# Old states of the sample group as the moving operand, with q spread out over zeros as the stationary one

## What is computed

```python
def step(s, inp):                       # s: old state (128 x 256) per sequence and head
    qc, kc, vc, gc = inp
    b = jnp.cumsum(gc, axis=1)
    ...
    o = (jnp.einsum('bhij,bjhv->bihv', a, vc)
         + jnp.einsum('bihd,bhdv->bihv', qc * jnp.exp(b), s))
    ...
o, s_new = _gla_chunked(q, k, v, glog, s0)      # 4 heads, key width 128, value width 256
o = o * lax.rsqrt(jnp.mean(jnp.square(o), -1, keepdims=True) + RMS_EPS) * gla_norm_w
o = o * jax.nn.silu(g)
```

## Time and profile before

| | us |
|---|---|
| median of 3 runs | 1268.34 (1265.9 to 1268.51) |
| the profiled execution's time | 1269.73 |
| its span, first to last instruction | 1268.0 |
| TensorE busy | 1162.3 (92%) |
| VectorE busy | 467.2 (37%) |
| ScalarE busy | 248.4 (20%) |
| HBM traffic | 454.50 MB moved, 358 GB/s over the span |
| mean granted TensorE clock | 0.991 |

### The profile page before, as it was taken

The page is one execution under the profiler, slowest core; times in us unless marked ns, Lnnn a source line. Parts: engine busy times, 40 slices in busy tenths (PEclk is TensorE's granted clock), DMA queues, the critical chain, the costliest instruction groups (busy, mean ns, idle before and its releaser), DMA issues.

```text
span 1268.0 us, 15570 instructions
## 1 busy us (share of the span) xinstructions
PE 1162.3 (92%) x6265; PEld 640.4 (50%) x6265; DVE 467.2 (37%) x796; ACT 248.4 (20%) x407; POOL 27.5 (2%) x44
## 2 busy tenths in 40 slices
PE   6999999999999999998898899989898988898884
PEld 6999999998543433433343234334333423343331
DVE  4575666665533232322222231223222222322135
ACT  4544344420211111111111111111111101110112
POOL 0000100100000000000000000000000000000001
PEclk9999999999899999999999999999999999999997
DMA  9526444692499999999999999999999999999993
GB/s 380 204 101 241 137 170 158 230 365 83 167 428 423 428 427 427 426 428 427 428 428 428 427 428 428 428 427 428 429 427 427 428 429 427 427 428 428 427 424 132
DMA packets 37945, 454.50 MB, mean 358 GB/s; under 512 B 4461, under 2 KB 4589, under 8 KB 9096
## 3 DMA queue, kind: packets, MB, share of 16 engines
q1 hardware_dynamic: 33744, 439.62, 83.0%
q0 software_dynamic: 4160, 14.29, 3.3%
HBM read 447.70 MB, written 6.31 MB: 358 GB/s over the span
## 4 chain that ended last, share of the span: by engine, by line
DMA 51%; PE 44%; DVE 3%; ACT 1%; issue 1%; SPq 0%; DVEq 0%; ACTq 0%
DMA ring<-in_w_gu 31%; DMA ring<-in_w_down 19%; PE bank L1009 13%; PE bank L706 12%; PE bank L1037 6%; PE bank L774 3%; PE bank L749 2%; PE bank L1061 1%; PE bank L982 1%; PE bank L833 1%; PE bank L820 1%; DMA ring<-in_w_mix 1%; PE bank L761 1%; DVE arena L1626 1%; PE bank L823 1%
## 5 line engine op out<-in xcount | busy, mean ns | idle before, releaser
L1009 PE MATMUL bank<-ring,arena 128*64 128x512 f32 x1504 | 339.8, 599 | 44.0 <-DMA ring<-in_w_gu 44.0
L1009 PEld LDWEIGHTS bank<-ring,arena 128*64 128x64 f32 x1504 | 103.7, 137 | 258.7 <-issue 182.8
L1037 PE MATMUL bank<-ring,arena 128*64 128x512 f32 x784 | 178.7, 598 | 18.0 <-DMA ring<-in_w_down 17.7
L706 PE MATMUL bank<-arena_r,ring_r 128*128 128x320 f32 x848 | 182.3, 316 | 0.0
L1865 DVE SCALAR_TENSOR_TENSOR arena_r<-bank,arena,arena_r 64x512 fp32r<-64x512 f32 x62 | 46.4, 749 | 289.5 <-ACT arena_r L1408 289.0
L706 PEld LDWEIGHTS bank<-arena_r,ring_r 128*128 128x128 f32 x848 | 138.7, 188 | 0.6 <-issue 0.4
L1828 DVE COPY arena<-bank 128x512 f32<-128x512 f32 x32 | 22.1, 692 | 290.6 <-PE bank L1009 290.6
L1009 PE MATMUL bank<-arena 128*64 128x512 f32 x528 | 119.8, 596 | 7.7 <-DMA arena<-in_w_gu 7.4
L1037 PEld LDWEIGHTS bank<-ring,arena 128*64 128x64 f32 x784 | 54.1, 136 | 121.9 <-issue 99.3
L1396 ACT ACTIVATE arena<-bank 128x512 f32<-128x512 f32 x32 | 19.1, 598 | 423.4 <-PE bank L1009 423.4
L1499 DVE TENSOR_TENSOR ring_r<-ring,ring_r 128x1024 fp32r<-128x1024 f32 x56 | 67.8, 1224 | 56.5 <-ACT ring_r L1225 56.3
(11 more groups left out here) (258 smaller groups left out, 957.8 us busy)
## 6 DMA issues: line engine op xcount, KB each, us to landing
ring<-in_w_gu SPq DMA_DIRECT2D x94, 2048.0 KB, 35.0
ring<-in_w_down SPq DMA_DIRECT2D x48, 2048.0 KB, 35.1
arena<-in_w_gu SPq DMA_DIRECT2D x33, 2048.0 KB, 35.2
ring<-in_w_mix SPq DMA_DIRECT2D x32, 1024.0 KB, 5.2
arena<-in_w_down SPq DMA_DIRECT2D x15, 2048.0 KB, 35.1
arena<-in_state_gla POOLq DMA_DIRECT2D x4, 1024.0 KB, 6.8
out<-arena POOLq DMA_DIRECT2D x4, 1024.0 KB, 5.6
alone<-in_w_gu SPq DMA_DIRECT2D x1, 2048.0 KB, 9.3
```

Of the source, the lines that this page charges most:

```text
L706: last = mm(o[:, 0:NT], w[a][:, c, f0:f0 + 128], rhs[b][:, c, :], start=c == 0 and a + b == 0, stop=c == chunks - 1 and a == 1)
L1009: last = mm(ex[i][side * CAP:(side + 1) * CAP, :], xgt[:, 2 * j + c, block * CAP:(block + 1) * CAP], w[:, c, i * D + side * 512:i * D + (s ...
L1037: last = mm(out[side * CAP:(side + 1) * CAP, :], actt[:, 4 * j + c, :], w[:, c, side * 512:(side + 1) * 512], start=j == 0 and c == 0, sto ...
```

## The change

The 64 small matmuls are taken out from between the chunks of the `g` products. In their place stands, behind the first `g` product of each head, a product `r` of its own: q of the 8 sequences is laid out by VectorE (`set_apart`) in a buffer of zeros, `q_apart`, so that sequence b has a block of 64 columns in which only its own 8 hold q. That block is the stationary operand (64 columns), the old state of the sequence with its 256 columns the moving one. Even sequences add up in partitions 0 to 63 of the bank, odd ones in 64 to 127. ScalarE copies the bank to SBUF (`old`), and one more matmul per half of the output (stationary 128 x 128 of `old`, moving `twice`: two 64 x 64 identity matrices one above the other) turns it and adds the two parts into the output's sample columns. The buffer of zeros lies in `alone`, so the first expert piece now waits for the last `r` and is issued behind all mixer units. `r` takes a place in `PRODUCTS`, so every bank number behind it moves on.

```diff
@@ PRODUCTS
-               [("o", h, 0), ("o", h, 1), ("g", 2 * h), ("kv", h, 0), ("kv", h, 1), ("g", 2 * h + 1)]
+               [("o", h, 0), ("o", h, 1), ("g", 2 * h), ("r", h), ("kv", h, 0), ("kv", h, 1), ("g", 2 * h + 1)]
@@ views
+        q_apart = alone[:, 0:B * NS]
+        old = reg(WRT, DV)
+        twice = reg(RMS + NT, NS)
@@ SyncE, mixer units
-                if n == 2 * RING:
-                    sp.dma_start(slot_view(-1), w_gu[0, 0, :, :]).then_inc(alone_in, 16)
@@ SyncE, behind the mixer units
+            sp.wait_ge(*full(("r", HEADS - 1)))
+            sp.dma_start(slot_view(-1), w_gu[0, 0, :, :]).then_inc(alone_in, 16)
             sp.wait_ge(stored_s, 16 * HEADS)
@@ TensorE, per head
             for h in range(HEADS):
                 outs = [claim(("o", h, vc)) for vc in range(2)]
+                weights_times("g", 2 * h, xt)
+                o = claim(("r", h))
                 pe.wait_ge(ss_in[h], 16)
-                def old_states(vc):
-                    def one(b):
-                        s0 = NP + b * L
-                        mm(outs[vc][:, s0:s0 + L], ss_st[h % 2][:, b, vc * 128:(vc + 1) * 128],
-                           q[:, h, s0:s0 + L], start=b == 0, stop=False, skip_group_check=True)
-                    return one
-                weights_times("g", 2 * h, xt, between=old_states(0))
+                pe.wait_ge(apart_ready, h + 1)
+                for i in range(B // 2):
+                    for g in range(2):
+                        b = 2 * i + g
+                        last = mm(o[g * NS:(g + 1) * NS, 0:DV], q_apart[:, b * NS:(b + 1) * NS], ss_st[h % 2][:, b, :],
+                                  start=i == 0, stop=i == B // 2 - 1)
+                last.then_inc(full(("r", h))[0], 1)
...
-                weights_times("g", 2 * h + 1, xt, between=old_states(1))
+                weights_times("g", 2 * h + 1, xt)
...
                 pe.wait_ge(sp_ready, 4 * (h + 1))
+                pe.wait_ge(old_ready, h + 1)
+                pe.wait_ge(twice_ready, 1)
                 for vc in range(2):
                     o = outs[vc]
                     f0 = h * DV + vc * 128
+                    mm(o[:, NP:NT], old[:, vc * 128:(vc + 1) * 128], twice, start=True, stop=False, skip_group_check=True)
@@ ScalarE, per head, ahead of the sigmoid of g 2h
+                act.wait_ge(*full(("r", h)))
+                A(old, bank(("r", h))[:, 0:DV], ACT.Copy).then_inc(old_ready, 1)
+                act.wait_ge(old_ready, h + 1)
+                act.sem_inc(freed(("r", h)), 1)
@@ VectorE
+            V.memset(q_apart, 0.0).then_inc(apart_zero, 1)
...
+            def set_apart(h):
+                V.tensor_copy(q_apart[:, 0:(B - 1) * (NS + L)].rearrange("p (b n) -> p b n", n=NS + L)[:, :, 0:L],
+                              q[:, h, NP:NT - L].rearrange("p (b s) -> p b s", s=L))
+                V.tensor_copy(q_apart[:, B * NS - L:], q[:, h, NT - L:NT]).then_inc(apart_ready, 1)
+            V.tensor_tensor(twice, ident[:, 0:NS], ident[:, NS:], ALU.add).then_inc(twice_ready, 1)
+            dve.wait_ge(apart_zero, 1)
+            dve.wait_ge(qk_ready, 4)
+            set_apart(0)
             for h in range(HEADS):
...
+                if h < HEADS - 1:
+                    dve.wait_ge(*full(("r", h)))
+                    set_apart(h + 1)
                 dve.wait_ge(sp_ready, 4 * h + 4)
```

More of the change, by code:

```diff
@@ L372, in build @@
         klm_ready = sem("klm_ready")
+        apart_zero = sem("apart_zero")
+        twice_ready = sem("twice_ready")
+        apart_ready = sem("apart_ready")
+        old_ready = sem("old_ready")
         kls_ready = sem("kls_ready")
@@ L693, in split, with weights_times @@
                 pe.wait_ge(split_ready, 2 * n + half + 1)
-            def weights_times(kind, i, rhs, chunks=KC, per_unit=2, between=None):
+            def weights_times(kind, i, rhs, chunks=KC, per_unit=2):
                 n = UNIT_NO[(kind, i // per_unit)]
@@ L702, in weights_times @@
                 for c in range(chunks):
-                    if between is not None:
-                        between(c)
                     for a, b in THREE:
```

## The result

The changed kernel takes 1283.9 us (median of 4 runs, 1281.67 to 1287.5), the kernel before 1267.12 beside it: a ratio of 1.0136, 95% interval 1.0108 to 1.0164. The forecast was 1274, with a range up to 1279.5: the right sign, and too little by a factor of 3 (16.8 us where 5.6 was forecast). In what follows every ratio compares medians with runs of the kernel before made beside it; one of the ten runs of experiment 1's kernel, 1984.07 us at a mean clock of 0.555, is a slow one and is left out of its ratio.

What follows compares the result with a forecast made beforehand. TensorE's path through the mixer heads, where VectorE's states set the output group's start, was taken to fix the expert stream's start. 2.2 us of added matmuls plus 3.4 of clock falls gave 5.6 on 1268.3: 1274 us, range 1269 to 1279.5.

Steps and rivals of the forecast that it cites:

- The path: Mixer to experts: a microsecond won or lost by TensorE in the mixer moves the expert stream and the end by one.
- `r` in the form of the samples' output projection: New product on TensorE: sixteen records, 1.77 us a head; 3.53 us if the halves don't overlap.
- The two matmuls of `old`: Output group, behind the wait for the states: 0.54 us a head with nothing to hide them.
- TensorE's standstill: Ahead of the output group: TensorE waits 1.9 us in heads 1 to 3 and 1.6 in head 0.
- ScalarE's order: Copy of `r` ahead of the sigmoid: hidden in heads 1 to 3, with 0.3 us to spare.
- The late first piece: First expert piece issued behind all mixer units: cost 0, thanks to a transfer gap; 4.9 us without the gap.
- The banks: Second `kvs` wants the first output half's bank one place earlier: costs nothing, as ScalarE has copied it by then.
- Head 0: First mixer head: TensorE's saving is eaten by ScalarE's new order; the loss is 0.54 us.
- the price of the clock: Clock falls in two of four heads at 1.70 us, from an expert-matmul row: 3.4 us; bounds 0 to 2.64 each.
- No fall: Rival: the clock stays up in all heads, only 2.2 us are lost, 1270.5 us; chance 0.27.
- Faster: Rival: VectorE's states come early enough, heads gain 1.25 us each, 5.0 in all, 1263.3 us; chance 0.10.
- No pairing: Rival: the halves of `r` don't overlap, 6.3 us more, 1276.8 us; chance 0.08, shared with a later ScalarE.

Runs made afterwards that it cites:

- experiment 1: Changed kernel with 12 throwaway projections ahead of TensorE's wait for the running states in each head: 1269.68 us, ratio 1.0025.
- experiment 5: Kernel before with only the first expert piece issued behind all mixer units: 1266.23 us, ratio 0.9999.
- Experiment 6: Changed kernel with 24 throwaway projections behind TensorE's waits, ahead of the output group, in each head: 1287.76 us, a single run without ratio.
- experiment 7: Changed kernel with, ahead of the wait, 6 throwaway projections (1271.41 us), 3 (1272.25 us), or the two `old` matmuls (1272.8 us); ratios 1.0034, 1.0046, 1.005.
- experiment 4: Changed kernel with VectorE's first silu and low part moved behind the four running states: 1263.49 us, ratio 0.9968.
- experiment 8: Changed kernel, running states early and `old` matmuls ahead of the wait: 1261.3 us, ratio 0.9956; control, kernel before with states early only: 1265.6 us, 1.0003.
- experiment 2: Kernel before without the 64 old-state matmuls and nothing in their place: 1281.98 us, ratio 1.012.

## Why the prediction fell short

**What held.** The path: the end hangs on the start of the stream (14.35 and 14.2 us). In heads 1 to 3 VectorE's states set the beginning of the output group, 12.68 us in the chain against 12.67. `r` in the form of the samples' output projection: 1.88 us for 1.77, halves in parallel. The two matmuls of `old`, 0.54 forecast: the period without a fall grew by 0.58 in experiment 1. TensorE's standstill: 1.86 us for 1.9 in heads 1 to 3; in head 0, 1.89 for 1.6. VectorE's low part in head 0: at 93.12 for 93.1. ScalarE's order hidden in heads 1 to 3. The late first piece: nothing (experiment 5). The banks: no wait for one is in the chain. And the sign. (The chances that the prediction adds up for "slower than 1270.9" give 0.765, where 0.74 stands.)

**Head 0** was forecast at 0.54 and is 25.66 us from its first `g` matmul (84.47) to ScalarE's high part at 110.13, against 24.63 before (84.61 to 109.24): 1.03. Of this 0.2 is the output group's start, which came through `r`, ScalarE's copy and high part and VectorE's states; 0.63 are the two matmuls of `old` (0.41 and 0.22).

**The step that failed** is the price of the clock, as the prediction put it: "I take a fall in two of the four heads at the 1.70 of the nearer row: 3.4 us". The mechanism was the right one and the likeliest case, but it was mis-sized twice. The profiled execution has three falls, not two. And a fall costs 4.5 us, not 1.70, outside even the upper bound of 2.64. Three times 4.5 are 13.5 us where 3.4 stood.

The sum of the profile closes: head 0 1.03, three periods 3 x (0.58 + 4.5) = 15.2, together 16.3, less the 0.14 by which head 0 began earlier; ScalarE's last table load of the heads is at 203.44 against 187.42, 16.0. By the start of the stream 1.7 of it is won back: the fall ahead of the experts, there before as well, lasted from 329.3 to 336.1 before and half as long now (clock 0.66 between 345 and 350):

```profile
345.00:350.00 5.00, 5.00 (x24) 2.60 (x24) 4.72 (x25) 2.13 (x3) 0.00 (x0) 0.66 0.00 2
```

The 16 records of the first expert piece take 4.79 us there, where they took 6.29: 1.5 of the 1.7.

Why was the price wrong? Both rows that it came from are of 512-column expert matmuls. There the clock was low for 3.4 us (1155) and 6.8 us (330). In the heads it was low for 10.2. The loss is the work done at the lower clock: TensorE's part of the chain of head 1 is 5.07 us longer, of which 0.6 is not the clock's. Experiment 6 puts dense matmuls in the same place: the same standstill gave 3.4 us of low clock and 1.5 us of loss, near the row's 1.70. Laid side by side, a fall of 3.4 us cost 1.5, one of 6.8 cost 2.9 (experiment 7), one of 10.2 cost 4.5: some 0.44 us for each microsecond of low clock, dense or narrow (the row of 1155 gives 0.5). So the row was right for a fall of its own length, and the falls of the changed kernel were three times as long. The prediction knew that narrow matmuls followed and used it for how likely a fall is, not for how long it lasts.

**The rivals.** No fall: experiment 1 is that case, 3.4 us above the kernel before beside it (1266.29) where 2.2 were forecast, inside the interval of 1.9 to 4.6. Faster: its condition, states that come earlier, was made in experiment 4. That its time, 1263.49, is almost the 1263.3 worked out is luck: the forecast started from 1268.3 and took off 5.0, the measured gain is 2.8 from 1266.29. In experiment 8, where no wait is left, it is 5.5, and 1.4 a head for the 1.25. TensorEngine Tiling (Array Packing), Performance Considerations, in the Trainium skill advises the exchange of operands; by the period of 24.29 us in experiment 8 the trace agrees, once TensorE is what the heads wait for. No pairing: out, by the 1.88 us.

**What stays open.** Which heads fall differs between kernels (not head 0 here; heads 0 and 2 in experiment 6), and the runs of the changed kernel spread over 5.8 us. The median is 16.8 us slower where the profiles show 14.2; that is because the profiled execution of the kernel before took 1269.73 us, 2.6 above its median, at a mean clock of 0.991 (most of its later runs have 0.993 to 0.996), while that of the changed kernel is at its median. That the length of a fall is set by what follows is argued, not shown: the two falls in front of dense matmuls in experiment 6 lasted 3.4 us, and all eleven in front of a narrow output group (experiments 2 and 7 and the changed kernel) 6.8 or 10.2, but no run shows why the same group had 6.8 once and 10.2 another time (experiment 2 has both), nor why the fall ahead of the experts was halved.

## What to carry to other kernels

Before taking work off TensorE, look whether it stands in the chain there: if it runs beside a longer chain on another engine, the saving becomes a standstill ahead of the meeting point, and a standstill can cost more than the work did (experiment 2: 64 matmuls fewer, 15.7 us slower). Move the other engine's deliverable forward first, or with it; here it took both, and neither alone was measurably faster. And price a fall of the clock by how long it lasts, which a row of another place does not tell: each microsecond of it cost some 0.44 us here.

## What the runs showed of the hardware

- A standstill of TensorE of 1.0 to 1.9 us, ahead of narrow fp32 matmuls (64 and 128 moving columns), was followed by a fall of the granted clock from 2.4 to 1.2 GHz in one to three of four heads (profiles of the changed kernel and of experiment 7). The same narrow group ran at the full clock in all heads of the kernel before, where TensorE's wait ahead of it was 0.2 us at most.
- At the lower level such matmuls take 1.8 times as long: 1.47 us for six records instead of 0.81.
- The low clock lasted 3.4 us in front of dense 320-column matmuls, 6.8 or 10.2 in front of the narrow group; the loss was 1.5, 2.9 and 4.5 us.
- Matmuls whose result nobody reads, put in a standstill, hold the clock: 48 of them, 7 us of work, made the program some 14 us faster (experiment 1).
